# A two-block transformer on one core: work moved at five places, and one-hots of 16 bits made for eight tokens at a time

## What is computed

```python
z = h @ w_in; u, v, g = split(z, 3)
v = layer_norm(v)                       # 16 groups of 128 columns
sv = einsum('gts,bcsgd->bctgd', wsm, v) + bs
h = h + (u * sv * silu(g)) @ w_out
h = h + (softmax_with_sink(q @ k_band) @ v_band * silu(gate)) @ w_out
```

```python
q = (h @ wq).reshape(T, 8, 2, 128)
sc = einsum('thpd,pnd->thpn', q, subkeys)          # 128 keys a side
top_v, top_i = top_k(sc, 16)
best_v, best_j = top_k(all sums of a pair, 16)      # of 128 * 128 experts
gates = softmax(best_v)
y[t] = sum over the token's 128 (head, place) of gate * gelu(x[t] . u[id]) * v[id]
```

## Time and profile before

| what | value |
|---|---|
| median of three runs | 1294.67 us (1293.56 to 1295.05) |
| profiled execution | 1295.06 us, its span 1292.9 us |
| PE busy | 97% |
| DVE busy | 76% |
| ACT busy | 59% |
| POOL busy | 30% |
| granted TensorE clock, mean | 0.994 |

### The profile page before, as it was taken

One profiled execution on the slowest core, in us unless ns is written; L12 is line 12 of the kernel. 1 busy time (PEld: TensorE's weight loads), 2 busy tenths in 40 slices (PEclk: granted clock), 3 DMA queues, 4 the chain that ended last, 5 costly groups with the idle time before them and its releaser, 6 DMA issues.

```text
span 1292.9 us, 26236 instructions
## 1 busy us (share of the span) xinstructions
PE 1254.3 (97%) x8596; PEld 1138.5 (88%) x8596; DVE 981.9 (76%) x1851; ACT 759.6 (59%) x1293; POOL 390.4 (30%) x254
## 2 busy tenths in 40 slices
PE   7989999999999989999999999999999999999997
PEld 7989999899999989999999888888888888888885
DVE  6999988897987767996999755556666666666666
ACT  6434445556766555558999644545555555555554
POOL 1179912225150147788888200000000000000000
PEclk9999999999999989999999999999999999999999
DMA  9978776453676245554434555556656566656662
GB/s 373 343 232 261 252 251 225 156 176 113 231 245 213 85 163 165 176 179 148 132 131 131 156 187 193 182 191 218 219 183 190 182 192 191 186 183 186 195 189 71
DMA packets 69344, 248.15 MB, mean 192 GB/s; under 512 B 7968, under 2 KB 8352, under 8 KB 68512
## 3 DMA queue, kind: packets, MB, share of 16 engines
q1 hardware_dynamic: 59920, 213.04, 51.1%
q10 hardware_dynamic: 9360, 34.27, 8.0%
HBM read 244.66 MB, written 2.62 MB: 191 GB/s over the span
## 4 chain that ended last, share of the span: by engine, by line
PE 61%; DVE 7%; ACT 5%; issue 2%; POOL 1%; DMA 0%; DVEq 0%; POOLq 0%; ACTq 0%
PE ps L2500 26%; PE ps L1931 11%; PE ps L2511 10%; PE ps L2513 5%; DVE O L1640 2%; DVE O L1631 2%; ACT WH L506 2%; PE ps L2339 1%; PE ps L2102 1%; DVE A L1617 1%; ACT A L912 1%; ACT O2b L906 1%; POOL tmp L1870 1%; PE ps L2121 1%; PE ps L2428 1%
## 5 line engine op out<-in xcount | busy, mean ns | idle before, releaser
L1025 DVE TENSOR_TENSOR WL<-raw,WH 128x1024 fp32r<-128x1024 f32 x320 | 408.5, 1282 | 86.0 <-ACT WH L506 81.8
L506 ACT ACTIVATE WH<-raw 128x1024 fp32r<-128x1024 f32 x392 | 411.4, 1053 | 64.5 <-PE ps L1931 30.7
L1931 PE MATMUL ps<-X,WH 128*128 128x256 f32 x1888 | 350.9, 287 | 1.4 <-DVE WL L1025 1.2
L1931 PEld LDWEIGHTS ps<-X,WH 128*128 128x128 f32 x1888 | 294.7, 192 | 2.2 <-DVE WL L1025 1.4
L1931 PE MATMUL ps<-X,WL 128*128 128x256 f32 x944 | 267.6, 283 | 0.0
L2511 PE MATMUL ps<-X,WH 128*128 128x512 f32 x576 | 205.5, 397 | 0.0
L2500 PE MATMUL ps<-WH,wvL 128*128 128x512 f32 x496 | 195.5, 394 | 0.0
L2500 PE MATMUL ps<-WH,wvH 128*128 128x512 f32 x496 | 195.3, 394 | 0.1
L2500 PE MATMUL ps<-WL,wvH 128*128 128x512 f32 x496 | 195.3, 394 | 0.0
L1897 POOL TENSOR_TENSOR WL<-raw,WH 128x1024 fp32r<-128x1024 f32 x72 | 173.6, 2415 | 59.1 <-ACT WH L506 59.0
L1931 PEld LDWEIGHTS ps<-X,WL 128*128 128x128 f32 x944 | 181.3, 192 | 0.0
(11 more groups left out here) (358 smaller groups left out, 2284.7 us busy)
## 6 DMA issues: line engine op xcount, KB each, us to landing
raw<-stream SPq DMA_DIRECT2D x392, 512.0 KB, 3.6
ada<-adaT ACTq DMA_DIRECT2D x47, 512.0 KB, 4.1
bias<-att_bias ACTq DMA_DIRECT2D x8, 512.0 KB, 4.7
x<-xT ACTq DMA_DIRECT2D x2, 512.0 KB, 5.8
raw<-stream SPq DMA_DIRECT2D x4, 256.0 KB, 6.0
ws<-wsT SPq DMA_DIRECT2D x1, 1024.0 KB, 8.4
lng<-rows SPq DMA_DIRECT2D x1, 1024.0 KB, 8.1
lnb<-rows SPq DMA_DIRECT2D x1, 1024.0 KB, 8.6
```

Source lines behind the costliest of these rows:

```text
L506: act.activation(WH[:, slot, :], raw[:, slot, :], ACT.Copy).then_inc(h_done, 1)
L1025: dve.tensor_tensor(WL[:, slot, :], raw[:, slot, :], WH[:, slot, :].bitcast(F32), ALU.subtract).then_inc(l_done, 1)
L1931: mm = pe.matmul(out_ap, a(kc), b(kc), start=(first and kc == 0 and i == 0), stop=(last and kc == KC - 1 and i == 2))
```

## The change

- Spatial groups: DVE makes the low half of C_UG + 3 between the two small and the two large normalising passes. POOL does groups 2 and 3 before the first two gate products.
- Attention: modulation tile 30 moves from the end of DVE's step 0 to the middle of step 1.
- Query norm: PE's gain broadcast moves behind the token sums, into banks 6 and 3; ACT copies it out after the second query copy, and stores the spilled rows later. The first query copy stands ahead of a conversion.
- Lists: PE turns them one projection earlier, and ACT and DVE take them up there. Indices are kept plus one, in 16 bits, and four rows of 256 are packed into one PSUM bank.
- One-hots: DVE makes them all, in four passes of 128x8 elements of 16 bits per round, tokens innermost, against a 16-bit counter that ACT wrote. POOL and ACT make none. PE reads both operands with a step of eight elements, and waits once for all of a round.
- Last projections: the last two tiles' halves and gelus stand ahead of the last conversion, and the last chunk is used before the one before it.

```diff
-        O1 = nc.alloc_sbuf_tensor_at("O1", [P, 8, NK], F32, offset=base_hot)
-        O2a = nc.alloc_sbuf_tensor_at("O2a", [P, 4, NK], F16, offset=base_hot + 8 * NK * 4)
-        gate_w = nc.alloc_sbuf_tensor_at("gate_w", [P, T], F32, offset=base_hot + 10 * NK * 4)
-        O2b = nc.alloc_sbuf_tensor_at("O2b", [P, 2, 4, NK], F16, offset=base_hot + 12 * NK * 4)
-        gate_h = gate_w[:, :].bitcast(F16).rearrange("p (t x) -> p t x", x=2)
+        hot_high, hot_low, hot_second, hot_eq, iota8 = (
+            nc.alloc_sbuf_tensor_at(name, [P, NK, 8], F16, offset=base_hot + i * NK * 16)
+            for i, name in enumerate(("hot_high", "hot_low", "hot_second", "hot_eq", "iota8")))
+
+        lists = nc.alloc_sbuf_tensor_at("lists", [P, 4, T], F16, offset=base_hot)
...
-        iota4 = iota.unsqueeze(1).broadcast_to([P, 4, NK])
-
-        def of_four(row, e, half):
-
-            return row[:, 8 * e + 4 * half:8 * e + 4 * half + 4].unsqueeze(2).broadcast_to([P, 4, NK])
+        def of_eight(k, e):
+
+            row = ps[:, 2, :].bitcast(F16)
+            return row[:, k * T + 8 * e:k * T + 8 * e + 8].unsqueeze(1).broadcast_to([P, NK, 8])
...
-            act.wait_ge(tr_mm, 1)
-            for i in range(2):
-                link.mark(act.activation(g2b[:, i * 512:i * 512 + 512], ps[:, 2 + i, :], ACT.Copy))
...
-            xtok_out(0, 2)
-            xtok_out(2, 3)
+            xtok_out(0, 1)
+            xtok_out(2, 2)
...
-            link.after(8)
-            act.dma_start(spill[:, 0:NT * D], xtok[:, :, :].rearrange("p t n -> p (t n)")).then_inc(spill_done, 16)
-            act.dma_start(spill[:, NT * D:NT * D + D], g2b[:, :]).then_inc(spill_done, 16)
...
-            for n in range(4):
+            qt_out(0)
+            hi(C_WQ + 3)
+            qt_out(1)
+            for i in range(2):
+                link.mark(act.activation(g2b[:, i * 512:i * 512 + 512], ps[:, (6, 3)[i], :], ACT.Copy))
+            hi(C_WQ + 4)
+            sc_out(0)
+            link.after(8)
+            act.dma_start(spill[:, 0:NT * D], xtok[:, :, :].rearrange("p t n -> p (t n)")).then_inc(spill_done, 16)
+            act.dma_start(spill[:, NT * D:NT * D + D], g2b[:, :]).then_inc(spill_done, 16)
+            for n in range(2, 4):
                 wq_step(n)
...
-            for j in range(TOP - 8, TOP - 1):
+
+            act.activation(iota8[:, :, :], iota.unsqueeze(2).broadcast_to([P, NK, 8]), ACT.Identity,
+                           bias=ones[:, 0:1]).then_inc(iota_ready, 1)
+            for j in range(TOP - 8, TOP - 2):
                 early_step(j)
+            act.wait_ge(lt_mm, 1)
+            act.activation(lists[:, 1, :], gate_l, ACT.Copy, scale=GATE_SCALE).then_inc(gate_high, 1)
+            early_step(TOP - 2)
             hi(C_U + 3 + TOP - 1)
-            act.wait_ge(lt_mm, 1)
-            act.activation(gate_h[:, :, 1], gate_l, ACT.Copy, scale=GATE_SCALE).then_inc(gate_high, 1)
-            act.activation(tmp[2][:, :], i2_l, ACT.Copy).then_inc(lt_ready, 1)
...
-            def hot_second(e):
-
-                o = O2b[:, e % 2, :, :].rearrange("p k n -> p (k n)")
-                act.wait_ge(dist_ready, e + 1)
-                act.activation(o, o, ACT.Square).then_inc(dist2_ready, 1)
-                act.wait_ge(dist2_ready, e + 1)
-                act.activation(o, o, ACT.Relu, bias=ones[:, 0:1], scale=-1.0).then_inc(hot2_ready[1], 1)
...
-            hot_second(0)
                 hi(C_U + TOP + 3 + e)
-                if e + 1 < ROUNDS:
-                    hot_second(e + 1)
...
-            column_step(LATE - 3)
-            for i in (LATE - 2, LATE - 1):
-                gelu(i)
-                w_high(i)
+
+            gelu(LATE - 3)
+            w_high(LATE - 3)
+            hi(NCHUNK - 2)
+            gelu(LATE - 2)
+            gelu(LATE - 1)
+            hi(NCHUNK - 1)
+            w_high(LATE - 1)
+            w_high(LATE - 2)
...
-            for cols in (slice(0, 2 * P), slice(2 * P, AW)):
+            def scaled(cols):
                 for t in range(NT):
                     dve.tensor_scalar(V[:, t, cols], V[:, t, cols], mv[:, 2 * t:2 * t + 1], rstd[:, t:t + 1],
                                       ALU.subtract, ALU.mult).then_inc(xhat_ready, 1)
+
+            scaled(slice(0, 2 * P))
             lo(C_UG + 3)
+            scaled(slice(2 * P, AW))
...
+                if m == 1:
+                    ada_tile(30)
...
-                if m < 8:
+                if 1 <= m < 8:
                     ada_tile(30 + m, g)
...
             dve.wait_ge(lt_mm, 1)
+            dve.tensor_scalar(lists[:, 3, :], i2_l, 1.0, None, ALU.add)
             dve.wait_ge(gate_high, 1)
-            dve.scalar_tensor_tensor(out=gate_h[:, :, 0], in0=gate_l, scalar=GATE_SCALE, in1=gate_h[:, :, 1],
+            dve.tensor_scalar(lists[:, 0, :], i1_l, 1.0, None, ALU.add)
+            dve.scalar_tensor_tensor(out=lists[:, 2, :], in0=gate_l, scalar=GATE_SCALE, in1=lists[:, 1, :],
                                      op0=ALU.mult, op1=ALU.subtract).then_inc(gate_low, 1)
             dve.wait_ge(gate_low, 1)
-            dve.tensor_copy(gate_l, gate_w[:, :]).then_inc(gate_packed, 1)
-            dve.wait_ge(lt_ready, 1)
+
+            dve.tensor_scalar(ps[:, 2, :].bitcast(U32), lists[:, :, :].rearrange("p k t -> p (k t)").bitcast(U32), 0, None,
+                              ALU.logical_shift_right).then_inc(gate_packed, 1)
+            dve.wait_ge(iota_ready, 1)
+            dve.wait_ge(gate_packed, 1)
...
-            def hot_first(e, half):
+            def hots(e):
                 if e >= 1:
-                    dve.wait_ge(gate_mm, 2 * e - 1 + half)
-                dve.tensor_tensor(O1[:, 4 * half:4 * half + 4, :], iota4, of_four(i1_l, e, half),
-                                  ALU.is_equal).then_inc(eq_ready, 1)
-
-            def hot_gated(e, half):
-
-                o = O1[:, 4 * half:4 * half + 4, :]
-                dve.wait_ge(eq_ready, 2 * e + half + 1)
-                if e == 0:
-                    dve.wait_ge(gate_packed, 1)
-                dve.tensor_tensor(o, o, of_four(gate_l, e, half), ALU.mult).then_inc(hot_ready, 1)
-
-            for e in range(ROUNDS):
-                hot_first(e, 0)
-                dve.tensor_tensor(O2a[:, :, :], iota4, of_four(i2_l, e, 0), ALU.is_equal).then_inc(hot2_ready[0], 1)
-                hot_gated(e, 0)
-                hot_first(e, 1)
+                    dve.wait_ge(hot_ready, e)
+                dve.tensor_tensor(hot_eq[:, :, :], iota8[:, :, :], of_eight(0, e), ALU.is_equal).then_inc(eq_ready, 1)
                 if e >= 2:
                     product_round(e - 2)
-                hot_gated(e, 1)
+                if e >= 1:
+                    dve.wait_ge(gate_mm, 2 * e)
+                dve.tensor_tensor(hot_second[:, :, :], iota8[:, :, :], of_eight(3, e), ALU.is_equal)
+                dve.wait_ge(eq_ready, e + 1)
+                dve.tensor_tensor(hot_high[:, :, :], hot_eq[:, :, :], of_eight(1, e), ALU.mult)
+                dve.tensor_tensor(hot_low[:, :, :], hot_eq[:, :, :], of_eight(2, e), ALU.mult).then_inc(hot_ready, 1)
+
+            for e in range(ROUNDS):
+                hots(e)
...
-                dve.wait_ge(wh_ready, up(EARLY + i + 1, g, 2))
+
+                dve.wait_ge(wh_ready, up(EARLY + i + 1 - (i == LATE - 1) + (i == LATE - 2), g, 2))
...
-            column_step(LATE - 3)
-            for i in (LATE - 2, LATE - 1):
-                gated(i)
-                w_low(i)
+            gated(LATE - 3)
+            w_low(LATE - 3)
+            lo(NCHUNK - 2)
+            gated(LATE - 2)
+            gated(LATE - 1)
+            lo(NCHUNK - 1)
+            w_low(LATE - 1)
+            w_low(LATE - 2)
...
             v_affine(0)
             v_affine(1)
             pool.wait_ge(xhat_ready, 4)
-            for n in range(2):
-                gate_product(n)
-                v_affine(n + 2)
+            v_affine(2)
+            v_affine(3)
+            gate_product(0)
+            gate_product(1)
...
-            pool.wait_ge(lt_ready, 1)
-
-            def distance(e):
-                if e >= 2:
-                    pool.wait_ge(gate_mm, 2 * e - 2)
-                pool.tensor_tensor(O2b[:, e % 2, :, :], iota4, of_four(tmp[2], e, 1), ALU.subtract).then_inc(dist_ready, 1)
-
-            distance(0)
-            pool_low(C_U + TOP + 2)
-            distance(1)
-            for e in range(ROUNDS):
-                pool_low(C_U + TOP + 3 + e)
-                if e + 2 < ROUNDS:
-                    distance(e + 2)
+            for e in range(ROUNDS + 1):
+                pool_low(C_U + TOP + 2 + e)
...
-            pe.wait_ge(diag_ready, 1)
-            for i in range(2):
-                mm = pe.matmul(ps[:, 2 + i, :], ones[:, :],
-                               diags[:, 4 * i:4 * i + 4, :].rearrange("p k n -> p (k n)"), start=True, stop=True)
-            mm.then_inc(tr_mm, 1)
...
+            pe.wait_ge(act_link, 3)
+            pe.wait_ge(diag_ready, 1)
```

(31 more changed lines are left out.)

8 lines of the change are left out of this document (3 added, 5 removed).

## The result

The changed kernel takes 1377.94 us (median of four runs, 1375.29 to 1380.1) against 1294.12 for the kernel before (four runs on the same chip, 1293.56 to 1295.05): a ratio of 1.0645, 95% interval 1.0631 to 1.0658. It is slower by 84 us, where about 15 us less was forecast. The profiled execution took 1380.1 us with a span of 1378.4.

A forecast was written before the change was run, and what follows sets the result against it. TensorE was busy 1254.3 of 1292.9 us; gate rounds were tied between VectorE and ScalarE. Terms 9.0 + 2.4 + 0 + 3.1 + 0.4 = 14.9 us took 1295.06 to about 1280 us (chance 0.62); range 1274 to 1300, its own 1275 to 1288.

The forecast's parts named there:

- The gate matmuls: Gate stage, TensorE: the same 16 matmuls a round, operands stepping 16 bytes, cost nothing more; slots stay 0.057 us.
- The upper bound: Gate matmuls: at most 2.2 times slower, the factor VectorE's gating pass pays for stepping a whole row.
- The rival that names the mechanism: Stepped operands slow 512 gate matmuls: 35 us at 2.2 times, 1315 us; outweighs the rest from 1.5 times; chance 0.12.
- VectorE's passes: Gate stage: four passes of 1024 16-bit elements at two per cycle, about 0.67 us each; late round 3.67 us, not 4.27.
- The rival of one element per cycle: VectorE's one-hot passes run at one element per cycle: rounds some 5.5 us, 53 us more, 1333 us; chance 0.09.
- Rounds bound by TensorE at 3.85 us: Gate stage: 32 rounds at TensorE's 3.85 us, 123.2 us, plus 0.4 for the stage.
- Single buffers and ScalarE's copy-out: Rival in the gate stage: they put VectorE's chain on the path, 4.0 us rounds; total 1285 to 1289; chance 0.13.
- Lists and rounds: Earlier list transposes and 3.85 us rounds, from last projection to first down matmul: 9.0 us gained, at worst 4.5.
- Spatial groups: Moved low half and affine steps remove waits of 1.2 and 2.91 us, new one later: net 2.4 us, between 0.5 and 4.0.
- Attention: Moving modulation tile 30 leaves the 1.44 us wait behind it: nothing gained, bounds 0.1 either way.
- Query norm: Gain broadcast leaves the path 1.6, less half clock 0.5, query copy earlier 1.0: together 3.1 us, from 1.5 to 4.
- Last projections: Two end waits, 0.7 us each with the pipeline's end, become one of about 1.0: gain 0.4 us, from 0 to 1.

The follow-up runs named there:

- The sweep: Changed kernel with gate matmul operands read at other steps every four rounds (wrong one-hots): slots 0.222 us at moving step 8, 0.054 contiguous, 0.064 at stationary step 8.
- pairs: Changed kernel with one-hots laid out 4 x 128 x 2, so TensorE steps two elements in both operands: 1281.49 us, ratio 0.9895; 1283.32 us in another set.
- fours kernel: Changed kernel with one-hots laid out 2 x 128 x 4, so TensorE steps four elements in both operands: 1311.96 us, ratio 1.013.
- The last experiment: The split, with ScalarE's pass that writes the repeated counter moved three early projections later: 1279.87 us, ratio 0.9882.
- The split: Pairs, with one half of the query norm's gain broadcast ahead of the token sums and the other behind them: 1281.0 us.
- contiguous: Changed kernel with both gate matmul operands read at a step of one element in all 32 rounds (wrong one-hots): 1280.81 us, ratio 0.9893.

## Why the prediction was right or wrong

**The gate matmuls: wrong, and this is nearly the whole error, 95.5 us of 98.** The step that failed is "I take nothing, being the nearest row by engine and type". The row was near by engine, type and shape, but not by operand: in the kernel before only the stationary operand steps, and the moving one is contiguous. A slot of 57 ns with a stepped stationary operand says nothing about a stepped moving one. The sweep shows how unlike they are: step 8 costs the stationary operand 10 ns a matmul and the moving one 0.168 us (0.222 against 0.054). The upper bound failed too. 2.2 times came from a VectorE pass with a step of a whole row, and the measured factor is 4.1 (0.235 against 0.057); another engine's price for a step is no bound. The rival that names the mechanism was there, with its break-even at 1.5 times, but at 35 us and a chance of 0.12.

What it cost can be summed from the rounds. After against pairs, 32 x (6.64 - 3.86) = 89.0 us. In six of the 32 rounds the projection behind the gate matmuls takes 4.08 to 4.14 us instead of 3.07, as in the window from 764.82 at a clock of 0.68 above: 6.4 together. That is 95.4, and the gate stages differ by 219.0 - 123.5 = 95.5.

The Trainium skill, "SBUF — State Buffer", paragraph on cachelines, had the direction right: a step of 16 bytes, one hit on each line, is slow. The trace agrees there (0.222 us against 0.054). By the same paragraph of the Trainium skill two hits on a line, which is a step of four elements here, are enough for full rate. The trace does not agree: they give half (0.111 us), and the read is proportional to the lines from a step of three elements on. By that limit the fours kernel would have been as fast as pairs; it is 30.5 us slower.

**VectorE's passes: right.** 1024 elements of 16 bits in 0.68 us, one operand in PSUM, four of them in a round. The rival of one element per cycle has fallen. Of the two pages of the Trainium skill, the perf-mode tier table of "VectorE: DVE Perf Modes" gives such a pass one element per cycle, and section 5.1 of "Vector Engine (DVE) Microarchitecture Reference" two. The trace agrees with section 5.1 (0.68 us for 1024 elements, 0.67 for 512 of 32 bits) and not with the table.

**Rounds bound by TensorE at 3.85 us: right, once the step is gone.** Pairs has 3.86 and a stage of 123.5 us; 123.2 and 0.4 were forecast. Single buffers and ScalarE's copy-out tie nothing: by its records TensorE is busy all 123.51 us.

**Lists and rounds, 9.0 us: 8.5.** From the first key scores to the first down matmul it is 249.7 us before (474.48 to 724.20) and 241.3 in pairs (470.86 to 712.12). The half microsecond missing stands around the wait of 0.30 us for a gelu, behind a pass of 1.13 us on ScalarE that the prediction did not cost: the one that writes the repeated counter. The last experiment gives it back, 0.55 us.

**Spatial groups, 2.4 us: about right.** Both old waits are gone, and the new one stands where it was worked out, at 82.00 for 82.1, though it is 1.21 us where 1.7 was worked out (82.1 less 80.4), and smaller ones stand before it: 0.54 us for GpSimd at 69.89 (not in pairs), 0.37 and 0.22:

```profile
70.97 0.50 PE L1926 MATMUL ps<-X,WH 128*128 128x256 f32 x2 [0.37 <-DVE WL L1023]
74.33 0.50 PE L1926 MATMUL ps<-X,WH 128*128 128x256 f32 x2 [0.22 <-DVE WL L1023]
...
82.00 0.51 PE L1926 MATMUL ps<-X,WH 128*128 128x256 f32 x2 [1.21 <-DVE WL L1023]
```

At the next norm, near 210 us, the kernels with the move are 0.9 to 2.8 us ahead of the two without (209.0 to 210.6 against 211.6 and 211.8), and undoing it costs 1.8 to 1.9 there and 1.2 to 3.0 by the medians.

**Attention, nothing: right.** The wait stays (1.44 before, 1.47 after), and from the norm ahead of it to its end it is 15.9 us in both.

**Query norm, 3.1 us: too much; 0.3 to 1.4 in the traces of pairs, -0.3 in that of the changed kernel (247.00 against 246.69).** Two steps failed. The broadcast was priced at 1.7 us in a stretch of which the text itself says that it runs at 0.79 of the clock; it lasts 3.56, 3.36 in pairs. And it was put beside the norm's small operations, which last 1.6 us, so it and the transposes behind it stand over their end by 2.9 (459.8 to 462.66). The query copy's gain came: its wait fell from 1.49 to 0.21 us, against a second wait of 0.95 for the normalised input. The split shows what the place was worth: 2.15 us more. Which of the two lengths of half clock an execution gets was no part of the forecast and is not explained here.

**Last projections, 0.4 us: 0.2**, one wait of 0.93 for the 1.0 forecast.

**The sum.** Without the step, the 14.9 us were 13.8 (contiguous), 13.1 and 11.4 (pairs, in two sets of runs). By stages the profiled execution of pairs has 2.2 (spatial), 1.4 (norm), 8.5 (lists and rounds) and 0.2 (end), 12.3 together; of what is short, the norm's term is the largest. That the contiguous kernel comes so near is in part luck: its runs are 1279.4 and 1279.6 at a mean clock of 0.999, 1282.0 and 1283.7 at 0.995. The terms' bounds, as they are written, add up to 1277 to 1289 and not to 1275 to 1288, which matters little. One term alone was wrong by some 95 us, the step of the moving operand, and its bound had been taken from another engine.

## What to carry to other kernels

When a layout is changed so that one engine can run through it (VectorE's innermost step of one), work out the step in bytes that TensorE's moving operand then sees: for 128 columns of 16 bits, four bytes are free here, and each further 2 bytes of step, up to 16, added half of the contiguous slot. Two elements innermost were enough for both engines. And a row bounds the cost of an access pattern only if it is of the same operand of the same engine; a free place on the path has to be priced at the clock granted in it.

## What the runs showed of the hardware that was not expected

- A moving operand of 16 bits and 128 columns: 0.054 us at a step of one element, 0.056 at two, 0.084, 0.111, 0.139, 0.166, 0.195 at three to seven, 0.222 at eight, 0.222 and 0.227 at twelve and sixteen; 1.74 ns for each 16 bytes touched. The contiguous 32-bit matmuls of 256 columns take a slot of 0.12 us, 64 pieces of 16 bytes, 1.9 ns each: near the same rate, so a step in them may cost at once; that was not tried. These are sums from the rounds' lengths, 2 to 5 ns under the mean distances of the starts.
- The stationary operand: a load record of 96 to 98 ns (medians) at steps of one and two elements, 113 at four and 145 to 148 at eight and sixteen, and a slot of 0.064 us. A contiguous one beside a moving operand that steps four elements or more has a record of 115 to 118 ns.
- TensorE's granted clock fell to half for 3.4 us (764.08 to 767.49 is one) in six rounds of the changed kernel, each fall 41 us behind the last, though its records leave no hole there. It did so in the sweeps only in the rounds with a moving step of eight elements or more (five of the 16 such rounds), in none of the other 48, and in no round of the contiguous, pairs and fours kernels. So the falls go with the slowly read operand; why they come in some such rounds and not in others is not shown. Most cost some 1.1 us.
